# Eight modulation chunks moved into the pause between two gather stretches, and TensorE adding every expert row of selections 20 to 47 and 160 to 319

## The reference, cut to what matters

```python
mod_x = (cond_x @ w_mod[l] + b_mod[l])[:, None, :]     # shifts, scales and gates, per layer
...
qr = (h @ wq).reshape(bsz, t, PEER_HEADS, 2, PEER_HALF)
scores = jnp.einsum('bthpd,hpkd->bthpk', qr, subkeys)
# two top-16 lists per head, their 256 sums, the top 16 of these -> eidx, gate
def block(args):
    hk, ek, gk = args
    act = jax.nn.gelu(jnp.einsum('ted,td->te', u[ek], hk), approximate=False)
    return jnp.einsum('te,ted->td', gk * act, v[ek])
```

## Time and profile before

| | us |
|---|---|
| median of three runs | 3643.84 |
| lowest, highest | 3640.47, 3649.80 |
| the profiled execution's own time | 3646.36 |
| span in that execution, first to last instruction | 3644.4 |

### The profile page before, as it was taken

The page is one execution under the profiler, slowest core; times in us unless marked ns, Lnnn a source line. Parts: engine busy times, 40 slices in busy tenths (PEclk is TensorE's granted clock), DMA queues, the critical chain, the costliest instruction groups (busy, mean ns, idle before and its releaser), DMA issues.

```text
span 3644.4 us, 36564 instructions
## 1 busy us (share of the span) xinstructions
PE 2721.3 (75%) x13210; PEld 1722.9 (47%) x13210; DVE 2700.4 (74%) x5470; ACT 764.3 (21%) x1535; POOL 960.6 (26%) x809
## 2 busy tenths in 40 slices
PE   6997499766766665676995766655477498998898
PEld 5866268432432222232682653311133175978596
DVE  4656978878788897677688668999987865546653
ACT  3211220110111110111101311111111144544263
POOL 0002223333343333444334014445334300000000
PEclk8999699887888778888997887876688699999999
DMA  8968789899999989999999549999999954545554
GB/s 299 377 226 323 274 324 388 314 398 357 379 375 378 394 337 368 413 364 381 347 381 378 189 190 404 392 370 370 376 392 422 359 214 151 185 168 202 179 196 150
DMA packets 278184, 1155.81 MB, mean 317 GB/s; under 512 B 20000, under 2 KB 21217, under 8 KB 179265
## 3 DMA queue, kind: packets, MB, share of 16 engines
q0 software_dynamic: 113344, 813.02, 56.2%
q1 hardware_dynamic: 162936, 334.76, 25.0%
q10 hardware_dynamic: 1736, 5.90, 0.4%
HBM read 1149.48 MB, written 4.13 MB: 317 GB/s over the span
## 4 chain that ended last, share of the span: by engine, by line
PE 40%; DVE 31%; DMA 19%; issue 5%; ACT 3%; POOL 1%; SPq 1%; POOLq 0%; DVEq 0%; ACTq 0%
DMA arena<-in_peer_uv,arena 14%; DVE arena L2931 10%; PE ps L1422 7%; PE ps L1339 5%; PE ps L994 5%; PE ps L996 5%; PE ps L995 4%; DVE arena L2955 4%; PE ps L1251 2%; PE ps L1386 2%; PE ps L1188 1%; PE ps L1496 1%; DVE arena L2803 1%; DVE arena L2806 1%; DVE arena L2812 1%
## 5 line engine op out<-in xcount | busy, mean ns | idle before, releaser
L1422 PE MATMUL ps<-arena 128*128 128x512 f32 x1696 | 1053.4, 762 | 640.6 <-DVE arena L2941 624.2
L3257 POOL DMA_INDIRECT arena<-in_peer_uv,arena x728 | 888.2, 1220 | 1482.8 <-PE ps L1422 734.4
L1422 PEld LDWEIGHTS ps<-arena 128*128 128x128 f32 x1696 | 372.9, 235 | 1226.5 <-DVE arena L2941 854.4
L2931 DVE CUSTOM_DVE_ANT_0 arena<-arena,hA 128x1024 f32<-128x1024 f32 x472 | 566.8, 1222 | 162.3 <-DMA arena<-in_peer_uv,arena 157.5
L2031 ACT ACTIVATE arena<-arena 128x1 f32<-128x1 f32 x768 | 154.9, 203 | 2039.4 <-DVE arena L2931 2038.6
L2931 DVE CUSTOM_DVE_ANT_0 arena<-arena,hB 128x1024 f32<-128x1024 f32 x256 | 308.8, 1223 | 140.8 <-DMA arena<-in_peer_uv,arena 138.5
L2404 DVE TENSOR_TENSOR w_lo<-ring,w_hi 128x1024 fp32r<-128x1024 f32 x220 | 265.2, 1224 | 167.5 <-ACT w_hi L1807 160.7
L2955 DVE SCALAR_TENSOR_TENSOR arena<-arena 128x1024 f32<-128x1024 f32 x299 | 382.4, 1279 | 0.5
L994 PE MATMUL ps<-hT_hi,w_hi 128*128 128x256 f32 x992 | 286.7, 289 | 16.9 <-DVE hT_lo L2412 14.7
L996 PE MATMUL ps<-hT_hi,w_lo 128*128 128x256 f32 x992 | 283.7, 286 | 0.0
L995 PE MATMUL ps<-hT_lo,w_hi 128*128 128x256 f32 x992 | 282.4, 285 | 0.0
(11 more groups left out here) (355 smaller groups left out, 3401.1 us busy)
## 6 DMA issues: line engine op xcount, KB each, us to landing
arena<-in_w_mod SPq DMA_DIRECT2D x43, 1024.0 KB, 9.7
ring<-in_w_in SPq DMA_DIRECT2D x16, 2048.0 KB, 21.3
ring<-in_w_mlp_in SPq DMA_DIRECT2D x64, 512.0 KB, 5.6
ring<-in_w_mlp_out SPq DMA_DIRECT2D x64, 512.0 KB, 5.6
ring<-in_peer_wq SPq DMA_DIRECT2D x12, 2048.0 KB, 20.4
ring<-in_w_mod SPq DMA_DIRECT2D x12, 2048.0 KB, 23.0
ring<-in_w_in SPq DMA_DIRECT2D x44, 512.0 KB, 7.6
hA<-in_w_mod SPq DMA_DIRECT2D x12, 1024.0 KB, 10.9
```

Of the source, the lines that this page charges most:

```text
L1422: mm = pe.matmul(ps[:, 6 + c, :], place(j)[:, 0:P], place(j)[:, D + c * CW:D + (c + 1) * CW], start=start, stop=stop)
L2931: dve.tensor_tensor_reduce(row, row, peer_buf[p][:, t, :], 1.0, 0.0, ALU.mult, ALU.add, dots[:, column(j):column(j) + 1]).then_inc(dot_don ...
L3257: pool.indirect_dma_start(place(j), None, A["peer_uv"], at).then_inc(uv_full[slot_of[j]], 16)
```

## The change

First, `PICKED` makes `on_pe` true for selections 20 to 47 and 160 to 319. Of these, 14 and 40 were added by VectorE.

Second, `plan_mod` gives the ring only 4 of the 12 chunks of layer index 2 (`MOD_RING`). The other eight are loaded in the pause as sixteen halves of 1 MB into buffers that are idle there (`gap_buf`, `GAP_IN`), each half after its buffer's last use (`gap_load`), multiplied by TensorE between its other work (`between` of the tensor block) and added to the bias by VectorE in two passes over 512 columns (`between` of the vector block). In the pause the second tile's output product moves behind the first tile's queries and scores; ScalarE copies the convolution half of that tile to `mixT`; GpSimd starts the second stretch only when all sixteen halves are multiplied. `forget` of the context takes its terms before the split of the next weights.

```diff
+        MOD_RING = 4
-            L_mod[l] = linear(chunked(A["w_mod4"][l]), 12)
+            L_mod[l] = linear(chunked(A["w_mod4"][l]), MOD_RING)
+        PICKED = [*range(20, 48), *range(SEG_END[1], SEG_END[2] + NQ)]
             w, t, n, seg = SELS[j]
+            if j in PICKED:
+                return True
...
+        GAP_IN = ["cs", "cg", "hA", "s2", "s3", "hB", "cs", "att", "s2", "s3", "hB", "sb", "s2", "s3", "cs", "hB"]
+            def gap_load(*halves):
+                for i in halves:
+                    b = GAP_IN[i]
+                    if gap_after[i] is not None:
+                        sp.wait_ge(mod_half, GAP0 + gap_after[i] + 1)
+                    elif b in ("cs", "cg"):
+                        sp.wait_ge(normed, NT * (norm_no["n_c1"] + 1))
+                    elif b == "hA":
+                        sp.wait_ge(tr_done, 4 * (turn_no["n_c1"] + 1))
+                    elif b == "att":
+                        sp.wait_ge(o_done, 5)
+                    elif b == "sb":
+                        sp.wait_ge(mix_ready, 5)
+                    else:
+                        sp.wait_ge(ring_done, L_in[2].g0 + 2 + 3)
...
             sp.wait_ge(gathers_sent, SEG_END[4] - 2)
-            weights(L_in[2])
+            chunk(L_in[2], 0, 0, 0)
+            chunk(L_in[2], 1, 0, 1)
+            gap_load(0, 1, 2)
             load_rows("r_x1")
+            load_rows("p_x1")
+            chunk(L_in[2], 2, 0, 2)
...
+            gap_load(3, 4, 5, 6, 7, 8, 9, 10)
+            sp.wait_ge(conv_done, 2)
+            sp.wait_ge(tile_mm, 3)
+            sp.dma_start(subk, A["subkT"][1]).then_inc(subk_in, 16)
+            gap_load(11, 12, 13, 14, 15)
+            for c in range(1, 4):
+                chunk(L_wq[2], c, 0, c)
...
+            def between(*chunks, bank):
+                for n in chunks:
+                    for h in range(2):
+                        i = 2 * (n - MOD_RING) + h
+                        b = GAP_IN[i]
+                        pe.wait_ge(gap_full[b], 16 * gap_turn[i])
+                        mod_products(bank, 1, lambda k: gap_buf[b][:, k % 4, :],
+                                     range(4 * h, 4 * h + 4), n % 4).then_inc(mod_half, 1)
...
+            between(4, bank=SUMS_7)
...
-            for c in range(2):
-                out_part(3, c, 1, CONV, True, False)
+            between(5, 6, bank=SUMS_7)
...
-            pe.wait_ge(mix_ready, 5)
-            for c in range(2):
-                out_part(3, c, 1, SCAN, False, True).then_inc(ring_done if c else out_mm, 1)
+            between(7, bank=SUMS_7)
+            between(8, bank=SUMS_8)
             turn_tile("p_x1", hA, 0)
             tile_turned("p_x1", 0)
             first_queries(2, 0)
             first_scores(2, 0)
+            between(9, 10, 11, bank=SUMS_8)
+            pe.wait_ge(mod_taken, PRO + 4)
+            pe.wait_ge(conv_done, 2)
+            pe.wait_ge(mix_ready, 5)
+            for c in range(2):
+                out_part(3, c, 1, CONV + SCAN, True, True).then_inc(ring_done if c else out_mm, 1)
+            pe.wait_ge(mod_taken, PRO + 8)
             turn_tile("p_x1", hA, 1)
...
+            def between(batch, bank):
+                dve.wait_ge(mod_half, GAP0 + 8 * (batch - 6))
+                dve.wait_ge(bias_in[batch % 2], 32 * (batch // 2 + 1))
+                for q in range(COLS):
+                    own = slice(q * 32, q * 32 + 2)
+                    ins = dve.tensor_tensor(mod_io[own, batch % 2, :], mod_io[own, batch % 2, :], ps[own, bank, :], ALU.add)
+                ins.then_inc(mod_taken, 4)
...
-                after(L, d)
+                if m != 2:
+                    after(L, d)
...
+                if j == SEG_END[4]:
+                    pool.wait_ge(mod_half, LATE0)
+                if j >= SEG_END[4] and slot_of[j] in (4, 5) and held_before[j] < SEG_END[4]:
+                    pool.wait_ge(out_mm, 3)
```

More of the change, by code:

```diff
@@ L843, in mod_load @@
                         sp.dma_start(half_buf[b], src.rearrange("(k p) n -> p k n", p=P)).then_inc(mod_full[b], 16)
-            def first_peer_weights(name, p, ahead):
-                load_rows(name)
-                for c in range(1, 1 + ahead):
-                    chunk(L_wq[p], c, 0, c)
-                if p == 0:
-                    sp.wait_ge(conv_used, 1)
-                else:
-                    sp.wait_ge(tile_mm, p + 1)
-                sp.dma_start(subk, A["subkT"][p // 2]).then_inc(subk_in, 16)
-                for c in range(1 + ahead, 4):
-                    chunk(L_wq[p], c, 0, c)
             def peer_weights(name, p):
@@ L891, in _ @@
             modulated(2)
-            first_peer_weights("p_c0", 0, 1)
+            load_rows("p_c0")
+            chunk(L_wq[0], 1, 0, 1)
+            sp.wait_ge(conv_used, 1)
+            sp.dma_start(subk, A["subkT"][0]).then_inc(subk_in, 16)
+            for c in range(2, 4):
+                chunk(L_wq[0], c, 0, c)
             load_rows("n_x0")
@@ L1186, in out_part @@
                 for k in ks:
-                    x = HV[:, k - HEADS] if k >= HEADS else mixT[:, k]
+                    x = HV[:, k - HEADS] if k >= HEADS and (m, t) != (3, 1) else mixT[:, k]
                     mm = pe.matmul(ps[:, 2 * ((L.e0 + c) % 2) + t, :], x[:, t * P:(t + 1) * P],
@@ L1862, in modulation @@
             def modulation(l):
-                for c in range(3, 12, 4):
+                for c in range(3, MOD_RING, 4):
                     yield MOD_AT[l] + MOD_STEP[l] * c + MOD_STEP[l]
@@ L2214, in _ @@
             take_score_tile(2, 0)
+            act.wait_ge(mod_taken, PRO + 4)
+            store(mod_io, 7)
             pick_exp((2, 0, 0))
+            act.wait_ge(mod_taken, PRO + 8)
+            store(mod_io, 8)
             turn_tile("p_x1", 1)
@@ L2389, in peer_entry @@
                 norm_tile(name, dst, 0, v)
+                if p == 2:
+                    between(7, SUMS_7)
                 for k in PICK_ORDER:
@@ L2392, in peer_entry @@
                         run(pick(k))
+                if p == 2:
+                    between(8, SUMS_8)
                 gated_tile(gate, L, dst, hA, 1, done)
@@ L2460, in late @@
                 ins.then_inc(late_taken, 1)
+            def between(batch, bank):
[5 more added lines that the diff above has]
+                ins.then_inc(mod_taken, 4)
             def modulation(l):
                 L = L_mod[l]
-                for c in range(12):
+                for c in range(MOD_RING):
                     yield MOD_AT[l] + MOD_STEP[l] * c + 2
```

26 lines of the change are left out of this document (21 added, 5 removed).

## The result

The median of five runs is 3627.02 us (3620.41 to 3632.73); the kernel before, five runs beside them, stayed at 3643.84 (3640.47 to 3651.11). The ratio is 0.9937, 95% interval 0.9922 to 0.9953: 0.6% faster, 23 us by the ratio, where 48 were forecast.

What follows compares the result with a forecast made beforehand. Bounds vary by stretch; in selections 160 to 319 transfers bound the middle, VectorE the end. Gains of 47 and 4 us less 3 make 48: 3646.4 becomes 3598.4, median 3596 us, range 3567 to 3628.

Steps and rivals of the forecast that it cites:

- Middle: Selections 160 to 319, 1091.0 to 1290.6 us: transfers bound and fall from 199.6 to 161.9; gain taken as 35 us.
- Both edits are needed: Middle of selections 160 to 319: without the moved adds VectorE, at 167.5 us, would bound instead of transfers at 161.9.
- End: 10: Selections 160 to 319, 1290.6 to 1420.4 us: VectorE bounds, falls from 118.2 to 106.8, idle unchanged; 10 us gained.
- Start: 2: Selections 160 to 319, 886.9 to 1091.0 us: transfers stay, VectorE loses 15.5 us beside them; 2 us gained (0 to 10).
- Selections 20 to 47: 4: 14 adds move: 11.3 us gained where VectorE bounds, 6.9 lost where TensorE bounds; 4 us gain taken.
- Cost: 3 us: Pause: chunk products, their sums and the last half's landing delay the output product; 3 us lost, bounds -3 to +20.
- the query chunks 1 to 3, first needed a pair later: Pause: these loads queue behind the halves on SyncE, but are first needed a pair later.
- Rival 3: Nothing gained: the engines' alternation sets the pace, selections 160 to 319 run at 333 GB/s; median 3653 us; chance 0.07.
- rival 1: Slots come back late because freed rows wait for TensorE; gathers run at 360 GB/s, median 3613 us; chance 0.17.
- Rival 4: Slower: TensorE at its lower clock, 7.56 us a pair against 6.67 in segment 2; median 3714 us; chance 0.05.
- Those for "right": Selections 160 to 319 about 486 us without line 2955, DMA share above 0.92, clock above 0.83; mixer projection 10 us sooner.
- those for "wrong": Gathers waiting mainly for TensorE's adds with DMA share under 0.88; a pause over 10 us longer, TensorE awaiting a half.

Runs made afterwards that it cites:

- experiment 3: Kernel before with modulation chunks 4 to 11 loaded to one quarter only, 12.6 MB less, compute instructions unchanged: 3646.21 us, ratio 0.9993.
- experiment 2: Changed kernel with the list of selections picked for TensorE emptied, so only the eight chunks are moved into the pause: 3647.21 us, ratio 0.9994.
- experiment 4: Changed kernel with the five pieces of each pick from pair 104 to 159 spread over seven pairs (one over six): 3603.73 us, ratio 0.9874.
- experiment 6: Changed kernel with TensorE adding only half the columns of each row of selections 160 to 287: 3609.88 us, ratio 0.9897.
- experiments 1 and 5: Kernel before with only the adds moved to TensorE, 3628.42 us; kernel before with only the picks of pairs 104 to 159 spread, 3627.17 us.

## Why the prediction was wrong

The direction and the range held; the size did not, 23 us of 48, for the most part because of one step, the first below. Its own steps, with selections 224 to 279 of every kernel as the ledger (us; idle is the stretch less VectorE's busy time):

| kernel | stretch | VectorE | idle | waits for gathers |
|---|---|---|---|---|
| before | 192.3 | 168.6 | 23.7 | 16.7 |
| loads of 4 to 11 a quarter | 189.9 | 168.4 | 21.5 | 14.6 |
| chunks alone | 181.9 | 162.6 | 19.3 | 12.8 |
| adds alone | 183.6 | 156.4 | 27.1 | 22.7 |
| adds alone, second profile | 184.7 | 155.7 | 29.0 | 24.6 |
| the change | 175.1 | 150.5 | 24.6 | 20.7 |
| the change, second profile | 174.2 | 150.3 | 23.9 | 20.0 |
| the change, half adds | 171.3 | 149.7 | 21.6 | 17.7 |
| before, picks spread | 181.4 | 168.1 | 13.2 | 3.1 |
| the change, picks spread | 161.9 | 149.5 | 12.4 | 8.5 |

- **Failed: "Middle: transfers fall from 199.6 to 161.9 us ... The larger holds, 161.9 ... 37.7 gained; I take 35."** The middle gained 17. It never took the larger of the two totals. Its time was VectorE's work plus some 20 to 29 us of idleness, most of it waits for gathers and most of those behind a run of picks, and the change cut only the first: 168.6 to 150.5, 18.1 us, of which the stretch got 17.2. The 16.8 MB of chunks, which the forecast priced at 43.1 us, were worth next to nothing (experiment 3: 32 us' worth of bytes away, ratio 0.9993); they had gone through in time that the stretch had to spare, by the reading above while the slots stood full. What the chunks' leaving did win from 224 to 279, 10.4 us by the chunks alone, is 6.0 less work of VectorE, its small sums, and the 2.4 of experiment 3; the other 2 us are not told apart (their matmuls leave TensorE too). A share of 0.97 was read as a bound. The sentence "a saving on VectorE alone, or on transfers alone, soon meets the other" named the alternation, and the sum then did not charge it.
- **"Both edits are needed" held for the stretch and not for the time.** From 224 to 279 the adds alone gain 8 to 9, the chunks alone 10, both 17 to 18: they add up, as savings of VectorE's work do. Over the kernel the adds alone give 0.9937, the chunks alone 0.9994, both 0.9937: what the chunks win in the stretch is lost again up to selection 543 (below).
- **"End: 10" was 6.3.** VectorE's work fell by 13.4 (118.2 to 104.8, more than the 11.4 forecast), but its idle time rose from 11.6 to 18.7, where it had been taken as unchanged. The same cause as in the middle.
- **"Start: 2" was -1.5.** VectorE's work fell 14.7 us and its idle time rose by 16.2; the transfers, at 0.95 and 376 GB/s, stayed as they were. That step was right, but for the 2 us that it took from the 5% in which the DMA engines rested.
- **"Selections 20 to 47: 4" was right.** From the first dot product to that of selection 160 passed 596.3 us before and 589.1 after: 7 gained, inside the bounds of -6 and 11; the second profile has 4.8. Its two halves show: at selection 42 the gain, counted likewise, was 14.7 (11.3 forecast; 11.1 in the second profile), and in the stretch that TensorE bounds it shrank, each pair there now costing 3.43 for two adds, as priced (2 x 1.72):

```profile
463.22 6.91 PE ps L1388 x32
470.12 3.43 PE ps L1471 x8
473.56 6.91 PE ps L1388 x32
```

- **"Cost: 3 us" for the pause was 5.6 (from 139.9 us between the dot products of selections 511 and 512 to 145.5; 146.2 in the second profile).** Counted from selection 511's dot product, the first tile's scores ended 1.6 us sooner (2 forecast). The last half took 7.58 us to land (6 forecast) and the output product 15.64 (13.8 forecast), which puts the product's end 3.4 us behind the forecast. The chain of waits in the pause after, against the earlier trace rows:

```profile
2103.40 1.16 PE ps L1262 x8
2104.56 1.03 PE ps L1137 x32
...
2105.60 7.58 DMA hB<-in_w_mod
...
2114.28 15.64 PE ps L1237 x32
...
2129.94 21.85 DMA ring<-in_peer_wq
```

  The last row is a step that the forecast called free, "the query chunks 1 to 3, first needed a pair later": the second chunk's place in the ring is freed by the product that the change moved back, so it was issued 6.7 us ahead of selection 512 and not 35.6. In the two profiles of the change TensorE then waited 0.6 and 0.8 us for it; in experiments 2 and 4 8.1 and 8.8.

  The pause itself went the other way. With the same program there, it took 140.5 us in experiment 2 and 141.8 in experiment 4, under the 3 us more that were forecast: the last half landed in 5.2 us in both, and the output product took 13.9 at a granted clock of 1.00. In the two profiles of the change the half took 7.58 and 6.89, and the product 15.6 and 15.7 at a granted clock of 0.89. TensorE had waited 4.2 and 3.5 us for the half there, against 1.8 in experiments 2 and 4. So the step that was mis-sized is the landing and the clock of the product behind it; the rest of the order cost what was forecast or less. From selection 511 to 544 the change cost 5.8 us (8.1 in the second profile), the chunks alone 9.3. With 2.8 lost from 320 to 511, that is where the 11.1 us that the chunks alone won in the stretch went.
- **The rivals.** Rival 3 had the mechanism (the engines' alternation sets the pace) though not its outcome, and rival 1 a part of it (experiment 6), but both prices were rates read from other stretches (333 and 360 GB/s; the stretch ran at 354). Their 0.24 of the chances was little for a pattern that the chain of waits showed. Rival 4 did not come: adds of 677 ns make 2.7 us for a row, 5.4 a pair, under 6.4 (511.5 / 80), and the clock rose to 0.91 over selections 160 to 319. The Trainium skill's page TensorE: Matmul & The Clock Gate (HAM oscillation — how this bites in real kernels) holds that a loop whose matmuls far outlast its waits stays at full clock, and one whose waits outlast its matmuls falls back. The rows agree in direction: in the middle 54.9 us of waits for diagonal matrices instead of 75.3, and 0.91 instead of 0.80. Experiment 6 is the reverse: half the columns, and 0.74.
- **The signs.** Those for "right" held in part: line 2955 was absent, the clock was 0.91, the mixer's first projection began 9.0 us sooner and that TensorE stretch ended 4.6 sooner, but the stretch took 511.5 us and the DMA share was 0.91. Of those for "wrong", the gathers did wait mainly for TensorE's adds (297.4 us), but they had done so before (228.8 us in selections 160 to 319), so this told nothing.

Shown by an experiment: that three quarters of the chunks' bytes cost nothing where they stood, that the adds carry the gain in time, that clustered picks cost 22 us in this stretch, and that the late query chunk costs the wait behind the pause. Only read from the rows, and not tried: more than six slots in the ring, which *S* says should do what the spread does. Also only read is what makes the wait for the query chunk 8 us in two kernels and under 1 in the changed one. The opening gathers of the second stretch stood further ahead of the chunk there: the first was issued 7.1 and 7.3 us before it, and six in all, against 2.9 and 3.0 us and three in experiments 2 and 4. Counted from that first gather, the chunk landed after 28.9 and 29.3 us in the change and 31.0 and 31.8 in the others.

## What to carry to other kernels

A stretch with two nearly equal totals need not take the larger of them. Where one side works in bursts that are longer than the buffer between the two (here five pairs of selections against slots for three), add to its work the idle time that its waits show at the end of each burst, and charge a saving against that sum; whether a deeper buffer would end this was not tried. A high DMA share is no bound while part of the transfers has slack: ask which transfer the chain names, and try the kernel with the suspected bytes left out before moving them. Spreading the bursts was worth as much as moving the work (22 and 23 us), and the two added up; it won nothing where the engine hardly waited. And when a product is moved back, look for the buffer that it frees.

## What the runs showed of the hardware

- The DMA engines carried gathers and weights together at 403 and 408 GB/s with a share of 1.00 and 1.01 (experiments 1 and 5), where 388 at 0.97 had looked full. The kernel before had itself carried 421 GB/s from 750 to 800 us and 426 from 2750 to 2800. The Trainium skill's page DMA: Bandwidth & Descriptors (Anatomy of one DMA — SWDGE (gpsimd) path) has bytes / 436 GB/s for the variable part; the 403 and 408 come within 8% of it.
- Half the columns did not halve a float32 add: 524 ns a record against 664, at a granted clock of 0.74 against 0.92. The work taken from TensorE came back in part as a lower clock.
- A 2 MB chunk of weights issued beside the opening gathers took 21.85 and 28.80 us to land, a 1 MB half into a quiet queue 7.58 and 5.19.
